# A convolution's sigmoid: one function of ScalarE, or its exponential and VectorE's reciprocal

## The reference, cut to what matters

```python
def conformer_conv_group(a, gate, w_dw, b_dw, ln_g, ln_b):
    u = a * jax.nn.sigmoid(gate)
    u = lax.conv_general_dilated(u, w_dw[:, None, :], ...) + b_dw    # 31 taps, each channel by itself
    return jax.nn.silu(layer_norm(u, ln_g, ln_b))                    # y * sigmoid(y), y = xc/std * ln_g + ln_b

def first_block(x, ...):
    proj = rms_norm(x, pre_mix_g) @ w_in
    a, gate, q, k, v = jnp.split(proj, splits, axis=-1)
    yc = conformer_conv_group(a, gate, ...)            # 256 tokens x 1024 channels
    ya = neighbourhood_attention_group(q, k, v, rpb)   # 16 heads, softmax over windows
    mix = jnp.concatenate([yc, ya], axis=-1) @ w_out
    ...                                                # then the MLP of the first block, and the second block
```

## Time and profile before

| | |
|---|---|
| median of 3 runs | 3024.66 us (3020.91 to 3025.14) |
| the profiled execution, by itself | 3019.02 us |
| its span in the profile | 3017.0 us |
| TensorE busy (matmuls) | 2609.3 us, 86% of the span |
| VectorE busy | 2157.1 us, 71% |
| ScalarE busy | 1421.6 us, 47% |
| GpSimd busy | 833.6 us, 28% |

### The profile page before, as it was taken

How to read it: one execution, slowest core, us unless ns; L and a number is a source line. 1 busy time by engine, 2 the same in 40 slices (tenths; PEclk the granted TensorE clock), 3 DMA queues, 4 the chain that set the end, 5 groups by cost and what they waited for, 6 DMA issues and landing times.

```text
span 3017.0 us, 36633 instructions
## 1 busy us (share of the span) xinstructions
PE 2609.3 (86%) x13064; PEld 2219.7 (74%) x13064; DVE 2157.1 (71%) x3298; ACT 1421.6 (47%) x2699; POOL 833.6 (28%) x564
## 2 busy tenths in 40 slices
PE   8999999999999999999999998777434008999997
PEld 6777878888888878898888897777333007888886
DVE  5996465454554565565546569999999988998888
ACT  5466454343443455545664442222299915333333
POOL 0000000010100000000000004766688865665553
PEclk9999999999999999999999999999755559999999
DMA  9544555555555556556435567999999997999997
GB/s 263 185 149 150 181 182 195 192 185 193 184 195 188 189 168 221 178 162 213 146 119 204 188 223 304 415 419 419 412 420 420 420 401 239 408 408 408 407 408 298
DMA packets 278956, 803.83 MB, mean 266 GB/s; under 512 B 33161, under 2 KB 81521, under 8 KB 245008
## 3 DMA queue, kind: packets, MB, share of 16 engines
q1 hardware_dynamic: 221216, 415.69, 40.8%
q0 software_dynamic: 57344, 385.91, 31.6%
q10 hardware_dynamic: 240, 0.18, 0.0%
HBM read 797.52 MB, written 4.19 MB: 266 GB/s over the span
## 4 chain that ended last, share of the span: by engine, by line
PE 69%; DMA 8%; POOL 8%; DVE 8%; issue 5%; ACT 1%; another core or an unknown queue 0%; SPq 0%; DVEq 0%; ACTq 0%; POOLq 0%
PE ps L240 15%; PE ps L241 15%; PE ps L242 15%; POOL expert_rows L2163 8%; PE ps L2707 7%; DMA expert_rows<-in_peer_u,index 5%; DVE conv L1361 2%; DVE wl L225 2%; PE ps L2714 2%; PE ps L2716 2%; PE ps L2715 2%; DMA expert_slabs<-in_peer_v 1%; PE ps L2249 1%; PE ps L2247 1%; PE ps L2248 1%
## 5 line engine op out<-in xcount | busy, mean ns | idle before, releaser
L225 DVE TENSOR_TENSOR wl<-ring,wh 128x1024 fp32r<-128x1024 f32 (+3 forms) x616 | 728.6, 1224 | 622.2 <-ACT wh L213 619.6
L213 ACT CAST wh<-ring 128x1024 fp32r<-128x1024 f32 (+3 forms) x612 | 603.1, 1035 | 622.8 <-PE ps L242 564.2
L2163 POOL DMA_INDIRECT expert_rows<-in_peer_u,index x256 | 478.0, 1867 | 579.1 <-DVE wl L225 419.6
L240 PE MATMUL ps<-wh,th 128*128 128x512 f32 (+2 forms) x1464 | 573.6, 392 | 5.3 <-DVE wl L225 5.3
L241 PE MATMUL ps<-wl,th 128*128 128x512 f32 (+2 forms) x1464 | 564.9, 386 | 0.0
L242 PE MATMUL ps<-wh,tl 128*128 128x512 f32 (+2 forms) x1464 | 564.8, 386 | 0.0
L2600 DVE CUSTOM_DVE_ANT_0 junk<-expert_rows,h 128x2048 f32<-128x2048 f32 x217 | 494.1, 2291 | 38.6 <-DMA expert_rows<-in_peer_u,index 36.5
L240 PEld LDWEIGHTS ps<-wh,th 128*128 128x128 f32 x1464 | 275.4, 188 | 63.6 <-DVE wl L225 7.7
L242 PEld LDWEIGHTS ps<-wh,tl 128*128 128x128 f32 x1464 | 275.2, 188 | 54.3
L241 PEld LDWEIGHTS ps<-wl,th 128*128 128x128 f32 x1464 | 275.5, 188 | 51.6
L2639 DVE SCALAR_TENSOR_TENSOR x_and_pieces<-expert_pieces,const,x_and_pieces 128x896 f32<-128x896 f32 x256 | 289.2, 1149 | 28.7 <-DMA expert_pieces<-in_peer_v,piece_index 15.0
(11 more groups left out here) (417 smaller groups left out, 4474.1 us busy)
## 6 DMA issues: line engine op xcount, KB each, us to landing
expert_slabs<-in_peer_v SPq DMA_DIRECT2D x128, 576.0 KB
ring<-in_w_in SPq DMA_DIRECT2D x64, 1024.0 KB, 5.2
ring<-in_w_up SPq DMA_DIRECT2D x64, 1024.0 KB, 5.1
ring<-in_w_down SPq DMA_DIRECT2D x64, 1024.0 KB, 5.0
ring<-in_w_in SPq DMA_DIRECT2D x68, 512.0 KB, 4.8
ring<-in_w_out SPq DMA_DIRECT2D x32, 1024.0 KB, 5.0
ring<-in_w_peer_q SPq DMA_DIRECT2D x16, 1024.0 KB, 5.2
ring<-in_w_in SPq DMA_DIRECT2D x16, 928.0 KB, 4.9
```

The costliest lines, as they stand in the source:

```text
L213: self.nc.scalar.copy(self.wh[:, i % 2, two, 0:w], self.ring[:, i, two, 0:w]).then_inc(self.high_ready, 1)
L225: self.nc.vector.tensor_tensor(self.wl[:, i % 2, two, 0:w], self.ring[:, i, two, 0:w], self.wh[:, i % 2, two, 0:w].bitcast(F32), ALU.subtr ...
L240: mm(o, hi, wh, start=start and k == 0, stop=False)
L2163: nc.gpsimd.indirect_dma_start(p.rows[:, n % GR, :], None, peer_u, bass.IndirectOffsetOnAxis(ap=p.index[:, n:n + 1], axis=0)).then_inc(p.l ...
```

## The change

The sigmoid is made as 1 / (1 + exp(-y)). ScalarE computes exp(-y), from the normalized values with a negated gain and bias; VectorE adds one and takes the reciprocal, in two halves of 128x1024. The exponentials go four at slab 37 and four at slab 38, behind the exponentials of that slab's head. VectorE's part goes at slabs 38 and 39, in place of 39 alone. The negated gain and bias are made once, when the vectors have been turned.

```diff
+    minus_both = core.small[:, 44:44 + 2 * CC]
+    minus_gain, minus_shift = minus_both[:, 0:CC], minus_both[:, CC:]
...
-        def sigmoids():
-            for c in range(CC):
-                act.wait_ge(normed, c // 4 + 1)
-                nc.scalar.activation(b.raw_sq[:, c, :], b.xc[:, c, :], ACT.Sigmoid, scale=core.v("conv_ln_g", c),
-                                     bias=core.v("conv_ln_b", c)).then_inc(sig, 1)
+        def decays(g):
+            act.wait_ge(rows_copied, 3)
+            act.wait_ge(normed, g + 1)
+            for c in range(4 * g, 4 * g + 4):
+                nc.scalar.activation(b.raw_sq[:, c, :], b.xc[:, c, :], ACT.Exp, scale=minus_gain[:, c:c + 1],
+                                     bias=minus_shift[:, c:c + 1]).then_inc(sig, 1)
...
-            if s == laid_at[-1] + 6:
-                sigmoids()
             if 23 <= s < 23 + HEADS:
                 exponents(s - 23)
+            if s in (laid_at[-1] + 6, laid_at[-1] + 7):
+                decays(s - laid_at[-1] - 6)
...
         def copy_taps():
...
+            dve.wait_ge(rows_copied, 2)
+            nc.vector.tensor_scalar(minus_both, core.v("conv_ln_g", 0, 2 * CC), -1.0, None, ALU.mult).then_inc(rows_copied, 1)
...
-        def swish():
-            for g in range(2):
-                dve.wait_ge(sig, 4 * g + 4)
-                dve.wait_ge(affine, 4 * g + 4)
-                tt(chunks(b.conv, g), chunks(b.conv, g), chunks(b.raw_sq, g), ALU.mult).then_inc(silu, 1)
+        def swish(g):
+            step = Steps(dve, stat_steps, 5 + 2 * g)
+            e = chunks(b.raw_sq, g)
+            dve.wait_ge(sig, 4 * g + 4)
+            step(nc.vector.tensor_scalar(e, e, 1.0, None, ALU.add))
+            step(nc.vector.reciprocal(e, e))
+            dve.wait_ge(affine, 4 * g + 4)
+            tt(chunks(b.conv, g), chunks(b.conv, g), e, ALU.mult).then_inc(silu, 1)
...
-            if s == 39:
-                swish()
+            if s in (38, 39):
+                swish(s - 38)
```

## The result

The change makes the kernel slower: the ratio of the runs is 1.0014, +0.14%, with a 95% interval of 1.0009 to 1.002. The medians are 3027.87 us (20 runs) against 3024.76 us (20 runs), 3.1 us or 0.10% apart. The forecast was 3028.8 us, +0.14%, and it called a change within 0.2% about what a measurement can't tell from none. Twenty runs of each do tell this one from none, for the interval leaves out 1.

The account below looks back on a forecast made before the run. TensorE bounds the kernel, waiting on ScalarE and VectorE: 3.6 us gained at slab 38, then VectorE's reciprocals and a clock fall put slab 40 4.1 us late; 3024.66 + 4.1 = 3028.8 us, range 3024.5 to 3033.

Parts of the forecast that it names:

- What goes from ScalarE: On ScalarE, two table loads of 1.28 us leave; head 14's turn comes at 272.37 us in place of 274.89.
- The price of the reciprocal: On VectorE, each 128x1024 reciprocal takes 6.53 us, at 6.23 ns an element from the 8- and 256-wide rows.
- The eight cycles: VectorE reciprocal by the skill page: eight cycles an element, 8.5 us for 1024, making the sum about 8 us.
- the dear rival: VectorE's reciprocal at 7.5 ns an element, 7.8 us at 1024: +6.7 us, 3031.4 us; chance 0.12.
- The cheap one: Rival: VectorE's wide reciprocal takes only 1.22 us, giving -2.2 us, 3022.5 us; chance 0.07.
- What stands behind swish(0): Split 39 and head 15's division queue behind VectorE's first-half add, reciprocal and multiply (8.44 us); TensorE idles 6.1 us.
- The clock's cost: TensorE's clock falls after the idle time ahead of head 15, costing 1.6 us before slab 40.
- With 1.6: Clock cost of 1.6 us, from peer-stage matmuls after a 2.27 us gap, putting slab 39 at 288.7, slab 40 at 296.3.
- its own row of 8.10 us of idle: Profile row of 32 peer-stage matmuls (L2742): 6.56 us after 8.10 us of idle, a clock cost of 2.7 us.
- the figure of 2.7: Rival of a clock low for longer, costing 2.7 us: +5.2 us; counted within the forecast's chance of 0.76.
- Two chains to slab 40: One over head 15's turn, one over the second half's multiply and split 40; both put slab 40 at 296.3, +4.1 us.
- The edits costed at nothing: Negation of gain and bias, about 0.2 us in VectorE's idle time, its satisfied wait, and SP's later slab 44 load: no cost.

Follow-up runs that it names:

- the run in pairs: Also called the run in four pieces: changed kernel with exponentials, add, reciprocal and multiply in pairs of channel groups, VectorE's over 128x512 at slabs 37, 38, twice 39; ratio 1.0004.
- the run with one load: Kernel before the change, with the eight sigmoids moved to slab 39 behind the last head's exponentials; 3019.48 us against 3025.26, ratio 0.9984.

## Why the prediction came out as it did

**What goes from ScalarE.** Right. The chain through ScalarE held; the turn of head 14 stands 14.00 us behind the mark, forecast 272.37 - 258.32 = 14.05. The exponentials with two columns took what the sigmoids had, 2.06 us for four.

**The price of the reciprocal.** Right: forecast 6.53 us, measured 6.55. Together with the run in pairs the groups by shape are these, first of the change, then of that run:

```profile
L1426 DVE RECIPROCAL sigmoids<-sigmoids 128x1024 f32<-128x1024 f32 x2 | 13.1, 6552 | 0.1
...
L1425 DVE TENSOR_SCALAR sigmoids<-sigmoids 128x1024 f32<-128x1024 f32 x2 | 1.4, 686 | 0.0
```

```profile
L1427 DVE RECIPROCAL sigmoids<-sigmoids 128x512 f32<-128x512 f32 x4 | 13.4, 3354 | 0.1
```

From 512 to 1024 elements it is 6.25 ns an element, much as from 8 to 256 (6.23). The eight cycles that I worked out from the Trainium skill's repeat count ("VectorE: DVE Perf Modes", First, the fixed hardware budget), an estimate of 8.5 us, don't show. Nor does the 7.5 ns that the widths of 2 and 8 gave, so the dear rival fell with both. The cheap one fell too.

**What stands behind swish(0).** Right: idle 6.10 us, forecast 6.1, and the division behind it released the wait. The table load's price is 1.28 us without a drain, again: in the run with one load, the copy ahead starts at 277.24 and lasts 0.58, the load begins at 277.84 and the sigmoids at 279.13. That is 1.29 us and not the 2.66 of "ScalarE: Activation LUTs", What ACT_TABLE_LOAD costs, in the Trainium skill.

**The clock's cost.** This term was mis-sized: "With 1.6" should have been 2.26, the figure that its own row of 8.10 us of idle (2.7) pointed to. The clock was low for longer, as the stretches of the change show (the restart is at 287.38):

```profile
285.00:285.50 0.50, 0.00 (x0) 0.72 0.00 0
...
291.50:292.00 0.50, 0.50 (x4) 0.50 0.00 0
292.00:292.50 0.50, 0.50 (x4) 0.95 0.00 0
```

From 287.38 to about 292.05 it ran at 1.2 GHz, 4.67 us, half of which is 2.3. I took the price of a gap of 2.27 us for one of 6. These 0.66 us, less 0.12 by which the turn of head 15 came earlier than forecast (26.21 us behind the mark, forecast 26.33), make up the 0.5 us between 4.1 and 4.59. At the figure of 2.7 that the prediction held ready as a rival, +5.2, the shift would have been forecast 0.6 us too high.

**Two chains to slab 40.** Both were there and within half a microsecond of each other, but they weren't equal: the one over head 15 decided. The second is 33.41 by the run without the first reciprocal, but that run's swish(1) starts earlier; in the change itself split 40 starts on ScalarE 35.60 us behind the mark (forecast 294.04 - 258.32 = 35.72). VectorE's part follows 1.07 later, and in the two runs where slab 40 waits for it TensorE starts another 1.38 and 1.37 us behind that, where the forecast had 1.24. This gives 38.05, 0.5 ahead of TensorE. The forecast had them 0.05 us apart mostly because its price for the clock was low.

**The edits costed at nothing.** The negation took 0.17 us at 39.20; VectorE then idles 1.65 us ahead of its next split, so it had the time. TensorE has no wait in the 45 us behind slab 40, so nothing waited for SP's load of slab 44.

**The end.** 4.59 us at slab 40 and 3.1 in the medians, whose runs spread over 7 us in the kernel before and 9 in the change: the interval, +2.7 to +6.0 us, holds both. So the medians don't confirm the size to a microsecond: that the forecast of 3028.8 us lies within 1 us of the median is in part luck, and the distance in the traces is the better witness.

## What to carry to other kernels

Ask of a function that moves between engines what is queued behind it on the engine that gets it, and who waits for that, not how busy the engine is. Here VectorE had time to spare, and one reciprocal of 6.55 us ahead of a 0.7 us division cost more than two table loads gave, while the same reciprocal a slab later added nothing to that, and 1.7 us where the first was gone. Before paying for a way around a table load, try where the function can stand so that the load hides or drops out: moving the sigmoids behind the last head, by which one load drops out, gave 4.3 us at slab 40. And let a measured distance reach past the last wait by a slab or more: the run in four pieces lost another 1.6 us just behind its end.

## What the runs showed of the hardware that wasn't expected

- What a fall of TensorE's clock costs follows from how long the clock is low behind the restart, and is a little under half of that: 1.20 us for 2.9 us at 1.2 GHz, 1.65 for 3.4, 2.26 for 4.7, 2.66 for 5.6. A longer idle time costs more by this (1.65 us after 2.88 of idle, 2.3 after 6.1, 2.66 after 12.64), but slowly.
- The clock can fall after the engine is back at work: 1.3 us behind the restart after 2.88 us of idle, 1.2 us behind it after 2.10. The rows of the wait itself then show no low clock.
- The length of an idle time doesn't tell by itself whether the clock falls. In the run in four pieces a wait of 2.10 us ahead of head 15 was followed by 2.4 GHz up to slab 40, and a second one of 2.10 us, 12 us later, by a fall that cost 1.6 us. Near 20 to 24 us the kernel before kept 2.4 GHz after 3.50 us of idle, while the nine other executions fell to 1.2 after 2.38 to 3.48. In the change this moved everything behind it by 2.85 us, about as much as the medians differ.
